# Two chained token-mixing blocks in split float32: where the low part of a weight tile is made, and when weights are cast and fetched at a stage's opening

## What is computed

```python
def hybrid_layer(x, pos, norm_g, w_in, ..., w_branch, w_out):      # first block, per layer
    h = rmsnorm(x, norm_g)
    proj = h @ w_in              # a_q a_k a_v a_f a_z  b_cq b_ckv b_kr b_z  c_q c_k c_v c_z  gates
    ...                          # three attentions, gated branches
    return x + merged @ w_out

def second_block(x, ...):
    for l in range(DEPTH):
        h = rmsnorm_2(x, mix_norm_g[l])
        x = x + token_mixers(h, ...)       # u = h @ w_in, four branches, gates, @ w_out
        h = rmsnorm_2(x, ffn_norm_g[l])
        x = x + (swiglu(h, ...) if l % 2 == 0 else moe_ffn(h, ...))
    return rmsnorm_2(x, final_norm_g)
```

## Time and profile before

| | us |
|---|---|
| median of 3 runs | 2499.84 |
| lowest, highest | 2493.63, 2500.19 |
| the profiled execution | 2493.18 |
| its span, first to last instruction | 2491.4 |
| PE busy in it | 2307.4 (93%) |
| DVE, ACT busy | 1754.3 (70%), 1299.3 (52%) |
| mean granted TensorE clock | 0.972 of full |

### The profile page before, as it was taken

One profiled execution on the slowest core, in us unless ns is written; L12 is line 12 of the kernel. 1 busy time (PEld: TensorE's weight loads), 2 busy tenths in 40 slices (PEclk: granted clock), 3 DMA queues, 4 the chain that ended last, 5 costly groups with the idle time before them and its releaser, 6 DMA issues.

```text
span 2491.4 us, 38137 instructions
## 1 busy us (share of the span) xinstructions
PE 2307.4 (93%) x14926; PEld 1958.9 (79%) x14926; DVE 1754.3 (70%) x2743; ACT 1299.3 (52%) x1886; POOL 18.3 (1%) x37
## 2 busy tenths in 40 slices
PE   6999988999998898799998899779999999999998
PEld 5988878988788877689988877677777777777776
DVE  4556675556687557674447547659889889898896
ACT  4545544545444433452234433347767767777674
POOL 0000000000000000000000000000000000000000
PEclk9999999999999999999999999979999999999998
DMA  5442334543373433255533533229999999999993
GB/s 160 144 137 87 102 119 127 155 126 115 113 172 120 154 95 108 90 182 168 188 119 120 154 100 105 99 103 397 349 343 358 350 349 355 346 359 348 345 356 134
DMA packets 255496, 488.82 MB, mean 196 GB/s; under 512 B 35112, under 2 KB 208072, under 8 KB 221400
## 3 DMA queue, kind: packets, MB, share of 16 engines
q1 hardware_dynamic: 249792, 483.87, 55.9%
q0 software_dynamic: 656, 1.71, 0.2%
q10 hardware_dynamic: 4872, 0.81, 0.2%
HBM read 485.30 MB, written 1.05 MB: 195 GB/s over the span
## 4 chain that ended last, share of the span: by engine, by line
PE 57%; DVE 10%; ACT 2%; issue 1%; DMA 0%; DVEq 0%; SPq 0%; ACTq 0%
PE bank L741 20%; PE bank L1107 14%; PE bank L765 10%; PE bank L580 5%; DVE memr L2044 3%; PE bank L549 3%; PE bank L504 1%; DVE mem_high L2532 1%; PE bank L481 1%; DVE mem_high L2574 1%; DVE mem_high L2578 1%; PE bank L779 1%; ACT memr L1577 1%; PE bank L749 1%; PE bank L1134 1%
## 5 line engine op out<-in xcount | busy, mean ns | idle before, releaser
L1107 PE MATMUL bank<-memr 128*128 128x256 f32 (+6 forms) x7440 | 955.7, 288 | 66.7 <-DVE memr L2044 29.5
L1107 PEld LDWEIGHTS bank<-memr 128*128 128x128 f32 (+3 forms) x7440 | 907.7, 187 | 106.8 <-DVE memr L2044 33.0
L969 DVE TENSOR_TENSOR memr_tail<-mem_tail,memr_ring 128x2048 fp32r<-128x2048 f32 x198 | 448.1, 2284 | 33.0 <-ACT memr_ring L837 31.4
L741 PE MATMUL bank<-memr_ring,memr 128*104 128x512 f32 x1492 | 463.3, 396 | 1.4 <-DVE memr L976 1.4
L2044 DVE TENSOR_TENSOR memr<-mem_low,memr 128x1024 fp32r<-128x1024 f32 (+3 forms) x328 | 389.5, 1203 | 89.8 <-ACT memr L1577 89.1
L1577 ACT CAST memr<-mem_low 128x1024 fp32r<-128x1024 f32 (+3 forms) x328 | 333.6, 1032 | 181.3 <-PE bank L1107 173.3
L837 ACT CAST memr_ring<-mem_tail 128x2048 fp32r<-128x2048 f32 x198 | 375.2, 1914 | 77.4 <-PE bank L741 46.7
L741 PEld LDWEIGHTS bank<-memr_ring,memr 128*104 128x104 f32 x1492 | 251.0, 168 | 93.7 <-issue 1.5
L765 PE MATMUL bank<-memr_ring,memr 128*104 128x512 f32 x752 | 243.6, 402 | 1.0 <-DVE memr L1025 1.0
L741 PE MATMUL bank<-memr_tail,memr 128*104 128x512 f32 x536 | 211.3, 394 | 0.0
L765 PEld LDWEIGHTS bank<-memr_ring,memr 128*104 128x104 f32 x752 | 125.3, 168 | 43.2 <-issue 1.2
(11 more groups left out here) (297 smaller groups left out, 2350.8 us busy)
## 6 DMA issues: line engine op xcount, KB each, us to landing
mem_tail<-in_moe SPq DMA_DIRECT2D x198, 1024.0 KB, 4.9
mem_low<-in_w_in SPq DMA_DIRECT2D x112, 1024.0 KB, 5.2
mem_high<-in_moe SPq DMA_DIRECT2D x33, 1024.0 KB, 4.8
mem_low<-in_moe SPq DMA_DIRECT2D x33, 1024.0 KB, 4.9
mem_high<-in_ffn_w SPq DMA_DIRECT2D x30, 1024.0 KB, 8.5
mem_low<-in_w_branch SPq DMA_DIRECT2D x20, 1024.0 KB, 5.0
mem_low<-in_w_out SPq DMA_DIRECT2D x16, 1024.0 KB, 5.1
mem_low<-in_w_in SPq DMA_DIRECT2D x6, 512.0 KB, 3.8
```

What stands on the lines that cost most here:

```text
L741: ins = pe.matmul(ACC[g % 2][0:CAP, :], h_[e % 2][:, kk, :], w_[:, 512 * k:512 * k + 512], start=(kk == 0 and i == 0), stop=(kk == KT - 1 ...
L969: TTn(raw_r[n % RAW], raw[n % RAW], hi_f[n % HI], ALU.subtract).then_inc(family("m_split"), 1)
L1107: ins = pe.matmul(out(bank), lhsT, rhs, start=((k, i) == order[0]), stop=((k, i) == order[-1]))
```

## The change

Eight things are edited.

1. `low_with(name)` and `cast_after`: at the openings DVE makes the low parts up to the casts that ACT does *with* the named unit, not only those before it, and some of these calls stand ahead of the normalisation.
2. `ahead` casts only when the named unit is the last user of its tile. Where two units share a tile, the cast comes after the second has been taken out.
3. In the first opening and that of the second mixer's layer 1 ACT makes all raw high parts first and squares afterwards; in the first opening the casts of tiles 0 and 1 stand between the raw parts and DVE makes their low parts ahead of the raw ones.
4. `gemm3_two` waits for each of its two tiles where it is first used.
5. In layer 1 of the first block and in both mixers of the second all eight casts of h come in one piece.
6. The table of Sqrt is loaded at the start, that of Tanh after `gk`.
7. After the MLP, SP fetches the next mixer's first chunk when the last but one of the MLP's up products is done, and the second chunk when the last is.
8. ACT casts those two chunks' tiles inside the MLP's last steps, and DVE ahead of the residual addition makes the low parts of the first chunk only.

```diff
-                for i in range(seen[0] + 1, tile + 1):
-                    pe.wait_ge(*at("w_split", i))
-                seen[0] = tile
                 two = [open_group(name) for name in names]
...
                     for name, bank, c0 in zip(names, two, cols):
+                        own = max(i for i in range(first, len(tiles)) if tiles[i][1] < c0 + m)
+                        if own > seen[0]:
+                            pe.wait_ge(*at("w_split", own))
+                            seen[0] = own
...
-            sp.wait_ge(*at("up1", NF - 1))
             for n in range(mid, len(chunks)):
+                if n < mid + 2:
+                    sp.wait_ge(*at("up1", NF - 2 + n - mid))
                 ring_chunk(n)
...
             def ahead(*name):
 
                 cast_before[name] = high_no[0]
-                if name in tile_of:
+                if name in tile_of and tile_use[tile_of[name]][1:] == name:
                     tile = tile_of[name]
                     high_parts(min(tile + 1 + AHEAD, min(e for e in phase_end[2:] if e > tile)), tile)
+                cast_after[name] = high_no[0]
 
             def follow(*name):
 
                 full(act, *name)
-                cast_before[name] = high_no[0]
-                if tile_use[tile_of[name]][1:] == name:
-                    ahead(*name)
+                ahead(*name)
...
+
+                st(A(raw[1][:, k, 0:n], src[:, k, 0:n], ACT.Identity, scale=pc(gain, k)), sig("h_high", key, k))
+
+            def square(key, src, k, n):
+
+                st(A(sq[:, k, 0:n], src[:, k, 0:n], ACT.Square), sig("squares", key, k))
+
             def raw_and_square(key, raw, gain, src, k, n):
 
                 if k == 0:
-                    st(A(stat[0:1, 1, 14:15], eps[0:1, 0:1], ACT.Sqrt))
+                    root_table()
                 if raw is not None:
-                    st(A(raw[1][:, k, 0:n], src[:, k, 0:n], ACT.Identity, scale=pc(gain, k)), sig("h_high", key, k))
-                st(A(sq[:, k, 0:n], src[:, k, 0:n], ACT.Square), sig("squares", key, k))
+                    raw_tile(key, raw, gain, src, k, n)
+                square(key, src, k, n)
...
             for l in range(DEPTH):
                 if l == 0:
+                    root_table()
                     act.wait_ge(*at("norm_gains", 0))
-                for k in range(KT):
-                    if l:
+                    for k in range(KT):
+                        act.wait_ge(*evacuated("xt", k))
+                        raw_tile(("raw", l), raw1, "norm_g0", x, k, TA)
+                        if k in (3, 5):
+                            high_parts(k // 2)
+                    high_parts(AHEAD)
+                    for k in range(KT):
+                        square(("raw", l), x, k, TA)
+                else:
+                    for k in range(KT):
                         full(act, "wo", l - 1, k)
                         if k < KT - 1:
                             follow("wo", l - 1, k)
-                    act.wait_ge(*(evacuated("wo", l - 1, k) if l else evacuated("xt", k)))
-                    raw_and_square(("raw", l), raw1, f"norm_g{l}", x, k, TA)
-                    if l and k == KT - 1:
-                        follow("wo", l - 1, k)
-                if l == 0:
-                    high_parts(AHEAD)
+                        act.wait_ge(*evacuated("wo", l - 1, k))
+                        raw_and_square(("raw", l), raw1, f"norm_g{l}", x, k, TA)
+                    follow("wo", l - 1, KT - 1)
...
-                    if j >= 3:
+                    if l and j == 2:
+                        high_some(range(KT))
+                    if l == 0 and j >= 3:
                         high_some(range(4 * j - 12, 4 * j - 8))
...
                     high_merged(j)
             def raw_mix(l):
 
-                if l == 0:
-                    act.wait_ge(*at("mix_gains_ready"))
+                if l:
+                    root_table()
+                    for k in range(KT):
+                        act.wait_ge(*at("mlp_added", 0, k))
+                        raw_tile(("mix_raw", l), raw2, f"mix_g{l}", x2, k, T)
+                    for k in range(KT):
+                        square(("mix_raw", l), x2, k, T)
+                    return
...
                         if l:
                             root_of_sum(XB, ("mix", l), 0, T)
                         else:
-                            high_some(range(4))
+                            high_some(range(KT))
                 if l:
-                    high_some(range(4))
+                    high_some(range(KT))
                 copy_unit(gla_q, ("gq", l), slice(0, P), scale=32 ** -0.5)
-                high_some(range(4, KT))
                 copy_unit(gla_k, ("gk", l), slice(0, P))
+                st(A(stat[0:1, 1, 14:15], eps[0:1, 0:1], ACT.Tanh))
...
@@ -1948,7 +1973,9 @@
                         if F + NHIGH < NF:
                             up_high(F + NHIGH, 0)
                             up_high(F + NHIGH, 1)
-                    act.wait_ge(*at("up1", NF - 1))
+                        if F >= NF - 2:
+                            act.wait_ge(*at("up1", F))
+                            high_parts(phase_end[DEPTH] + 2 * (F - NF + 3))
...
                 low_until(tile_of.get(name, -1) + 1)
@@ -2067,22 +2096,27 @@
                                           op0=ALU.add, op1=ALU.mult), free("z", l, j))
                 low_after("z", l, j)
 
-            low_until(AHEAD - 1)
+            low_until(2)
+            for k in range(KT):
+                raw_low(("raw", 0), raw1, "norm_g0", x, k, TA)
+            low_until(AHEAD)
             for k in range(KT):
                 add_square(("raw", 0), k, TA)
             for l in range(DEPTH):
                 m0 = first_row(l)
                 if l == 0:
-                    low_after("cq", l, 0)
-                    low_after("cq", l, 1)
+                    low_with("cq", l, 1)
+                else:
+                    low_with("wo", l - 1, KT - 1)
                 normalise(at("root_done", 0, ("raw", l)), 0, f"norm_g{l}", x, h, range(KT), lambda k: sig("h_raw", l, k))
-                low_after("cq", l, 0)
-                low_after("cq", l, 1)
-                for j in (2, 3):
-                    for k in range(4 * j - 8, 4 * j - 4):
-                        low_h(l, k, TA)
-                    low_after("cq", l, j)
-                low_after("cq", l, 4)
+                low_with("cq", l, 2)
+                if l == 0:
+                    low_with("cq", l, 3)
+                for k in range(KT):
+                    low_h(l, k, TA)
+                    if k == 3:
+                        low_with("cq", l, 3)
+                low_with("cq", l, 4)
...
                 if l:
                     for k in range(KT):
                         raw_low(("mix_raw", l), raw2, f"mix_g{l}", x2, k, T)
+                    low_until(phase_end[DEPTH] + AHEAD)
                     for k in range(KT):
                         add_square(("mix_raw", l), k, T, ("mix", l))
-                    low_after("rq", l, 0)
-                    low_after("rq", l, 1)
+                    low_with("rq", l, 1)
+                else:
+                    low_with("wo", DEPTH - 1, KT - 1)
                 norm2(("mix", l), f"mix_g{l}" if l else "final_mix_g", lambda k: sig("h_raw", ("mix", l), k))
-                low_after("rq", l, 0)
-                low_after("rq", l, 1)
-                low_after("rk", l, 0)
-                for k in range(4):
+                low_with("rk", l, 0)
+                for k in range(KT):
                     low_h(("mix", l), k, T)
-                low_after("rk", l, 1)
-                for k in range(4, KT):
-                    low_h(("mix", l), k, T)
-                low_after("gq", l)
+                    if k == 3:
+                        low_with("rk", l, 1)
                 for i, nm in enumerate(("cos64", "sin64")):
                     st(TTn(turned[:, i, :], const(nm)[:, 0:T], rstd[:, 0, 0:T], ALU.mult))
                 dve.wait_ge(*evacuated("gq", l))
                 st(TTn(gla_q, gla_q, rstd[:, 0, 0:T], ALU.mult))
-                low_after("gk", l)
+                low_with("gq", l)
                 dve.wait_ge(*evacuated("gk", l))
...
-                    low_until(phase_end[2] + AHEAD)
+                    low_until(phase_end[DEPTH] + 2)
```

23 lines of the change are left out of this document (12 added, 11 removed).

## The result

| | before | changed |
|---|---|---|
| median of 4 runs, us | 2499.19 | 2476.18 |
| lowest, highest | 2493.63, 2500.19 | 2473.39, 2479.05 |
| the profiled execution | 2493.18 | 2476.70 |
| its span | 2491.4 | 2474.9 |
| mean granted TensorE clock | 0.972 | 0.969 |

The ratio is 0.9915, with a 95% interval of 0.9901 to 0.9929: 21 us less by the ratio, 23 by the two medians (2480 was forecast, in a range of 2463 to 2495). The kernel before has one run more here than in its own table. The two profiled executions lie only 16.5 us apart: that of before was faster than all four runs timed, 6.0 under their median, and that of the changed kernel stands 0.5 above its own.

The account below looks back on a forecast made before the run. PE, 93% busy, was taken as the bound. Gains of 38.6 us less losses of 9.3 and 10.6 gave 18.7 less: 2474.5 from the profiled execution, 2481.1 from the median, taken as 2480, range 2463 to 2495.

Parts of the forecast that it names:

- First opening, 12.4: First block, layer 0: PE starts 4.4 us earlier, stops before the fifth cq unit go, matmuls run faster; 12.4 us less.
- Layer 1's opening, 9.7: First block, layer 1: stops of 2.16, 4.69 and 0.76 go and 48 matmuls take 2.1 less; 9.7 us less.
- The DVE chain that I feared: First block, layer 1: DVE's low parts end at 411.0, PE wants them at about 412.1; a margin of 1 us.
- Shared tiles at `mq` and `mk`, 1.5 a layer: Later casts at mq's and mk's shared tiles remove short PE stops: 1.5 us per layer, 3.0 in two layers.
- Second mixer's opening, 4.9: Second mixer, layer 0: stops of 1.58 and 1.47 go, and nearly all of 2.08; 4.9 us less.
- MLP into layer 1, 8.6: Second mixer, behind the MLP: PE starts 3.55 earlier, first 48 matmuls take 3.0 less, later stops shrink; 8.6 us less.
- the rival in which the early fetch does nothing: Behind the MLP: the slot is held until the last product; 3.6 less gain, 2484; no separate chance, within the forecast.
- What edit 2 costs in the middle, 9.3: Second mixer's middle: new stop of 2.7 before gz6, later mqk casts, lower clock; 4.1 and 5.2, together 9.3 us lost.
- Around the scans, 10.6: Second mixer: two low parts fall behind DVE's scans, delaying the third gate unit; 5.3 us per layer, 10.6 lost.
- The rival that DVE would bound the openings: Openings of the first block's layer 1 and the second mixer give half; net 7.1 less, 2493; chance 0.22.
- the slower one: Openings of both blocks: low parts ahead of the normalisation hold it up; +9, 2509; chance 0.07.
- The rival in which the middle would not mind: Second mixer's middle: new waits fall into PE's existing idle stretches; net -38.6, 2461; chance 0.10.

Follow-up runs that it names:

- run 6: Kernel before with only the first opening's new order (ACT, DVE and gemm3_two, layer 0 of the first block): ratio 0.9957 to before.
- run 12: Changed kernel with DVE's eight raw low parts again ahead of the first tiles' low parts in the first opening: ratio 0.9928 to before.
- run 9: Changed kernel with DVE's weight low parts in the first block's layer 1 placed as before, ACT's order as changed: ratio 0.9921 to before.
- run 10: Changed kernel with ACT's casts of h in the first block's layer 1 in two pieces again, DVE's places as changed: ratio 0.9926 to before.
- run 5: Changed kernel with the old rule of ahead for the second mixer's middle alone, the new rule elsewhere: ratio 0.9832 to before, 2455.7 us.
- run 8: Changed kernel with raw part and square made in turn again in the second mixer's layer 1, behind the MLP: ratio 0.9931 to before.
- run 11: Run 5's kernel with the low part of the 1152-wide tile made ahead of gate gz 4: ratio 0.9811 to before, 2449.4 us.
- run 2: Changed kernel with the old rule of ahead and follow everywhere, cast_after kept: ratio 0.9868 to before.
- run 7: Changed kernel without the slot-by-slot fetch behind the MLP; raw parts first and squares last as changed: ratio 0.9925 to before.
- run 3: Kernel before with only the rule that ahead casts at a tile's last user: ratio 1.0053 to before.
- run 1: Changed kernel with DVE making the low parts of the two tiles cast with the second gv unit ahead of the scans: ratio 0.9882 to before.
- run 4: Changed kernel with the old rule for the xbc and mv units only, so gz6's tile is cast ahead of mv 0's copy: ratio 0.9886 to before.

## Why the prediction was right, point by point

**First opening, 12.4: right.** 13.0 without the input's 0.8. Start 4.4 forecast, 5.1 found (15.85), 4.3 of it not the input's; runs 6 and 12 confirm it. The wait of 0.6 for h's low parts did not come.

**Layer 1's opening, 9.7: the size right (10.9), the reason too narrow.** I named DVE's places; runs 9 and 10 show that for the largest stop ACT's single piece or DVE's place would each have done. The DVE chain that I feared ended with h's last low part at 395.12 + 1.49 = 396.6, and `fq` started at 397.05 without a wait.

**Shared tiles at `mq` and `mk`, 1.5 a layer: right.** The shift there was 1.5 in layer 0 (-13.75 to -15.21) and 1.4 in layer 1 (-24.83 to -26.21). The table has only 0.2 and 0.9 at the next opening, since some groups behind the place ran slower, but that is this one execution's: in runs 5, 8, 10 and 11, which have the same order in this stage, 1.5 to 1.7 of layer 0 were left.

**Second mixer's opening, 4.9: 5.7.** That the stop of 2.08 was edit 2's is shown by run 2; that edits 1 and 5 removed those of 1.58 and 1.47 is read from the order of the lists, no run undid them there. Nor did a run undo edit 4 or 6 by itself.

**MLP into layer 1, 8.6: 9.3.** The start gave 3.3 of 3.55 (run 7: 3.3), the 48 matmuls 2.7 of 3.0 (run 8: 2.6); the rival in which the early fetch does nothing falls with run 7. The load of ACT's table took 1.28 and the next instruction began 0.02 us behind its end (1276.01 and 1277.31 in the timeline), so no drain was to be paid for. The prediction was right in this, but not by its row: in the trace of before ACT's next instruction came at 1300.45, 0.57 behind the load's end, and waited for DVE. The loads at 861.63 and 863.66 of that trace show it, each followed within 0.02.

**What edit 2 costs in the middle, 9.3: mis-sized, 12.3.** The new stop was 2.67 (2.7 forecast) in each layer. What I had too small is the clock: behind it layer 0 lost 1.6 and layer 1 2.8 (18.68 and 19.88 for 144 matmuls that take 17.11 at full clock, in run 9 below). My sum holds 1.5 for each layer (5.2, and 4.1 = 5.2 - 1.1), though its words add it in layer 1 alone. The later stop in layer 0 did not shrink: 2.63, with 7.41 for 48; so the 1.1 I had given back stayed lost. In layer 0 the 144 matmuls took 18.4 us or more in every trace with this stop (19.91 in run 3). In layer 1 the excess is partly chance. Runs 9, 10 and 12 have the same instructions and the same stop there; run 9:

```profile
1353.70 17.11 PE L1108 MATMUL bank<-memr 128*128 128x256 f32 x144 [2.67 <-DVE memr L2069]
...
1382.60 7.45 PE L1108 MATMUL bank<-memr 128*128 128x256 f32 x48 [2.27 <-DVE memr L2069]
```

Here the clock stayed full behind the first stop and fell behind the second, where the changed kernel's trace has it the other way round (19.88 and 5.89). In all three this middle cost 5.6 against the kernel before, and not 6.8: near the 5.2 forecast.

**Around the scans, 10.6: 11.9.** The mechanism was right to the instruction; the cold unit took 5.49 and 5.28 rather than 4.4. Run 1 shows that the place of two low parts on DVE is the cause: with them ahead of the chain the unit waits 2.12, as before (2.17), and over the stretch 4.9 and 4.8 of the 11.9 come back at once; what stays, 1.1 and 1.2, goes with slower matmuls (8.44 for 48, 7.34 before). DVE stood idle for 8.49 us just ahead of the scans, with both casts done at 834.1: it took nothing out of its listed order, as the Trainium skill's strict first in, first out has it ("TensorE: Matmul & The Clock Gate", Architectural detail: the array is 16x 32x32, not 1x 128x128). Listed there, they ran there (run 1, 833.23).

**The sum.** Gains 40.7 found (38.6 forecast), losses 24.3 (19.9): 16.5 less by the traces, 18.7 forecast. So two misses of 2.1 and 4.4 stand against each other, in part. That the median came within 4 us of 2480 is in part luck of the clock: the medians differ by 23, 6.5 more than the two traces that this account explains. The rival that DVE would bound the openings is refuted by all three of them, and the slower one by the reciprocal at 28.67. The rival in which the middle would not mind is refuted by runs 1 and 4.

## What to carry to other kernels

A rule that decides for every shared buffer when the next fill may start is worth testing place by place: here "only at the last user" won 1 to 4 us at some places and lost 10 to 12 a layer at others, and the kernel with each form in its place is 20 us faster than with the new rule everywhere and 9 to 10 faster than with the old one (runs 5 and 2). When a producer follows its consumer's release by a noted count, check whether the count is taken before or after the release: work noted one step late can land behind a long chain on an in-order engine. A stop ahead of PE costs its length and then, in some executions and not in others, what the next groups run at a lower clock; both have to stand in the sum, the second as a range.
